# Nine projection tiles of a gated-linear-attention layer, computed by tokens in Strassen's scheme with GpSimd forming the weight sums

## The reference, cut to what matters

```python
def gla_branch(h, w_in, w_gate_up, gate_bias, out_norm_w):
    q, k, v, r, z, xq = split_cols(h @ w_in, [512, 512, 2048, 16, 3072, 1024])
    g = log_sigmoid(r @ w_gate_up + gate_bias) / 16
    o = gla_chunked(q * 128 ** -0.5, k, v, g)     # 4 heads, causal, state 128 x 512
    return rms_norm_2(o, out_norm_w), z, xq

# per layer:
xa = memory_attention(xq, mem_n, w_kv)
y = concatenate([seq_out, xa], -1) * silu(z)
x = x + y @ w_out
```

## Time and profile before

| | us |
|---|---|
| median of 3 runs | 1570.79 (1570.35 to 1570.9) |
| the profiled execution's own time | 1573.19 |
| its span, first to last instruction | 1571.4 |
| PE busy | 1522.5 (97%) |
| DVE busy | 656.8 (42%) |
| ACT busy | 288.3 (18%) |
| POOL busy | 82.2 (5%) |

### The profile page before, as it was taken

One profiled execution on the slowest core, in us unless ns is written; L12 is line 12 of the kernel. 1 busy time (PEld: TensorE's weight loads), 2 busy tenths in 40 slices (PEclk: granted clock), 3 DMA queues, 4 the chain that ended last, 5 costly groups with the idle time before them and its releaser, 6 DMA issues. The chain is left out here.

```text
span 1571.4 us, 22409 instructions
## 1 busy us (share of the span) xinstructions
PE 1522.5 (97%) x9037; PEld 973.5 (62%) x9037; DVE 656.8 (42%) x1262; ACT 288.3 (18%) x550; POOL 82.2 (5%) x125
## 2 busy tenths in 40 slices
PE   6999999999999999999999999998999999899998
PEld 2475655434434443443445788887888887488887
DVE  2544324111111111112311213473788888895663
ACT  2222202111212111112121020101232232240000
POOL 0000000000000000000100000001122122000000
PEclk9999999999999999999999999998999999999999
DMA  9544639899999999999333243334344344233441
GB/s 398 210 161 161 269 131 417 336 422 422 422 422 422 422 421 422 421 422 414 118 115 119 95 161 139 129 134 164 135 167 166 138 154 178 98 135 127 164 168 50
DMA packets 53889, 376.03 MB, mean 239 GB/s; under 512 B 7216, under 2 KB 18224, under 8 KB 19264
## 3 DMA queue, kind: packets, MB, share of 16 engines
q1 hardware_dynamic: 53536, 374.02, 59.9%
q10 hardware_dynamic: 288, 1.11, 0.2%
HBM read 373.99 MB, written 1.11 MB: 239 GB/s over the span
## 5 line engine op out<-in xcount | busy, mean ns | idle before, releaser
L1246 PE MATMUL ps<-ring,x_gathered 128*64 128x512 f32 x1024 | 227.4, 597 | 0.9 <-DVE x_gathered L1311 0.9
L1320 DVE TENSOR_TENSOR act_slots<-gate,ps 64x512 f32<-64x512 f32 x32 | 22.1, 690 | 380.8 <-ACT gate L1284 380.8
L2203 PE MATMUL ps<-hT,ring 128*128 128x256 f32 x768 | 173.6, 385 | 1.8 <-PEq L115 1.8
L1246 PEld LDWEIGHTS ps<-ring,x_gathered 128*64 128x64 f32 x1024 | 74.0, 138 | 148.3 <-issue 148.3
L2203 PEld LDWEIGHTS ps<-hT,ring 128*128 128x128 f32 x768 | 146.0, 193 | 23.8 <-issue 4.1
L1269 PE MATMUL ps<-ring,act_turned 128*64 128x512 f32 x512 | 116.9, 598 | 0.0
L1764 PE MATMUL ps<-hT,ring 128*128 128x256 f32 x512 | 111.4, 379 | 0.0
L1764 PEld LDWEIGHTS ps<-hT,ring 128*128 128x128 f32 x512 | 97.0, 190 | 14.7 <-issue 1.7
L1759 PE MATMUL ps<-ring,hT 128*128 128x512 f32 x192 | 85.6, 604 | 2.1 <-PEq L115 2.1
L1269 PEld LDWEIGHTS ps<-ring,act_turned 128*64 128x64 f32 x512 | 33.9, 136 | 79.1 <-issue 54.8
L1224 PE MATMUL ps<-y,selT 64*128 64x512 f32 x264 | 75.0, 634 | 0.7 <-ACT y L1290 0.7
(11 more groups left out here) (597 smaller groups left out, 2054.6 us busy)
## 6 DMA issues: line engine op xcount, KB each, us to landing
ring<-in_experts SPq DMA_DIRECT2D x192, 1024.0 KB, 15.7
ring<-in_weights SPq DMA_DIRECT2D x75, 2048.0 KB, 7.9
b_raw<-in_s_b SPq DMA_DIRECT2D x16, 128.0 KB, 7.1
s_a_rows<-s_ab_rows SPq DMA_DIRECT2D x64, 32.0 KB, 6.5
c_raw<-in_s_c SPq DMA_DIRECT2D x16, 128.0 KB, 6.1
b_by_state<-in_s_b_by_state SPq DMA_DIRECT2D x16, 128.0 KB, 2.0
x<-in_x ACTq DMA_DIRECT2D x1, 1024.0 KB, 4.9
mix_room<-in_mem SPq DMA_DIRECT2D x1, 1024.0 KB, 14.1
```

The costliest lines, as they stand in the source:

```text
L1246: last = pe.matmul(h_ps[rows, :], xg[:, f, :], w[:, kk, m, :], start=(f == 0), stop=(f == KD - 1))
L1320: dve.tensor_tensor(act_s[:], gate[:], h_ps[upper, :], ALU.mult).then_inc(act_ready, 1)
L2203: last = pe.matmul(out[:, f, :], w[:, kk, (2 * h + f) * P:(2 * h + f + 1) * P], rhs[:, kk, :], start=(kk == 0), stop=(kk == KD - 1))
```

## The change

Tiles 1 to 9 of the GLA projection are computed by a new class `TokenTiles`, by tokens, in Strassen's scheme. Tile 0 stays a plain tile by tokens, tiles 10 to 13 stay by features. The method `dve_weights` is renamed `sum_weights` and takes an engine; for the nine tiles that engine is POOL, for the other Strassen tiles it stays DVE.

```diff
+class TokenTiles(Strassen):        # fresh = 3, weight sums in zT, row sums in gla_xqT
+    def dve_rows(self, dve):
+        dve_row_sums(dve, self.rows_of(), self.row_sums).then_inc(self.rows_ready, 1)
+    def pe_first(self, pe, i):
+        self.k.wait_tile(pe, self.first + i)
+        pe.wait_ge(self.rows_ready, 1)
+        pe.wait_ge(self.weights_ready, i)
+        if i > 1:
+            pe.wait_ge(self.c11_out, i - 1)
+        self.pe_products(pe, i, 0, ("p1", "p6"), True).then_inc(self.part_done, 1)
+        if i > 1:
+            pe.wait_ge(self.rest_out, i - 1)
+        self.pe_products(pe, i, 1, ("p7", "p5"), True).then_inc(self.part_done, 1)
+    def pe_second(self, pe, i):
+        pe.wait_ge(self.u2_out, i)
+        self.pe_products(pe, i, 0, ("p2",), False).then_inc(self.part_done, 1)
+        pe.wait_ge(self.c22_out, i)
+        self.pe_products(pe, i, 1, ("p4", "p3"), False).then_inc(self.k.tile_done, 1)
+    def act_p1(self, act, i):
+        act.wait_ge(self.part_done, 3 * i - 2)
+        act.activation(self.one, self.ps(0, 0), ACT.Copy).then_inc(self.p1_out, 1)
+    def act_c11(self, act, i):
+        act.wait_ge(self.part_done, 3 * i)
+        act.activation(self.quarters(i)[0], self.ps(0, 0), ACT.Copy).then_inc(self.c11_out, 1)
+    def dve_u2(self, dve, i):
+        dve.wait_ge(self.p1_out, i)
+        dve.tensor_tensor(self.two, self.one, self.ps(0, 1), ALU.add).then_inc(self.u2_out, 1)
+        dve.drain()
+    def dve_c22(self, dve, i):
+        dve.wait_ge(self.part_done, 3 * i - 1)
+        dve.tensor_tensor(self.three, self.two, self.ps(1, 0), ALU.add)
+        dve.drain()
+        dve.tensor_tensor(self.quarters(i)[3], self.three, self.ps(1, 1), ALU.add).then_inc(self.c22_out, 1)
+    def dve_rest(self, dve, i):
+        dve.wait_ge(self.k.tile_done, self.first + i + 1)
+        dve.tensor_tensor(c21, self.two, self.ps(1, 0), ALU.add)
+        dve.tensor_tensor(c12, self.two, self.ps(1, 1), ALU.add).then_inc(self.rest_out, 1)
+        dve.drain()
```

Banks 6 and 7 hold [128, 256] twice each. `pe_products` issues 4 matmuls of 256 columns per product. In the lists of the engines:

```diff
 # tensor
-                half(2)
-                half(3)
-                half(4)
+                pe.wait_ge(out_dve, 2)
+                tiles.pe_first(pe, 1)
+                tiles.pe_second(pe, 1)
+                tiles.pe_first(pe, 2)
                 pe.wait_ge(g_ready, 1)          # then L1805 to L1809
...
-                half(5)
-                half(6)
-                half(7)
+                tiles.pe_second(pe, 2)
+                tiles.pe_first(pe, 3)
+                tiles.pe_second(pe, 3)
                 pe.wait_ge(dec_ready, 1)        # then the transposes of q and k
...
-                half(8)                         # before the scores
+                tiles.pe_first(pe, 4)
...
-                for i in range(9, 12):
-                    half(i)
+                tiles.pe_second(pe, 4)
+                tiles.pe_first(pe, 5)
+                tiles.pe_second(pe, 5)
                 pe.wait_ge(att_ready, 1)
-                pe.wait_ge(out_act, 12 - DVE_HALVES)
+                pe.wait_ge(tiles.c11_out, 5)
+                pe.wait_ge(tiles.rest_out, 5)
...                                              # updates, first(6), intra(0), second(6), intra(1), inter(1)
-                half(14)
-                for i in range(15, 22):
-                    half(i)
+                for i in range(7, TM_END):      # TM_END = 10
+                    tiles.pe_first(pe, i)
+                    tiles.pe_second(pe, i)
+                half(20)
+                half(21)
                 for r in range(2):
-                    pe.wait_ge(o_normed, 1)
+                    pe.wait_ge(gated, r + 1)
 # gpsimd
+                for i in range(1, TM_END):
+                    tiles.sum_weights(pool, i)
                 pool.wait_ge(summed, 8)         # the reciprocal root of o
 # scalar
+                tiles.act_p1(act, 1)
                 act.wait_ge(abs_ready, 1)
                 act.activation(lg, lg, ACT.Exp, scale=-1.0)
                 act.drain()
                 act.activation(lg, lg, ACT.Ln, bias=1.0).then_inc(log_ready, 1)
-                take(4)
+                tiles.act_c11(act, 1)
+                tiles.act_p1(act, 2)
...
-                for i in range(5, 16):
-                    take(i)
+                tiles.act_c11(act, 2)
+                for i in range(3, 8):
+                    tiles.act_p1(act, i)
+                    tiles.act_c11(act, i)
...                                              # squares of o, then p1(8), Silu of z tiles 6 to 9 in place,
...                                              # with c11(8), p1(9), c11(9) among them
 # vector
+                tiles.dve_rows(dve)              # first in the list
                 take(0)
...
-                take(2)
+                tiles.dve_u2(dve, 1)
                 dve.wait_ge(log_ready, 1)
                 ...                              # L1965, L1967 -> g_ready
-                take(3)
+                tiles.dve_c22(dve, 1)
+                tiles.dve_rest(dve, 1)
+                tiles.dve_u2(dve, 2)
+                tiles.dve_c22(dve, 2)
                 dve.wait_ge(exp_done, 1)
                 dve.scalar_tensor_tensor(out=q, in0=q, ..., in1=eq[:], ...)
+                tiles.dve_rest(dve, 2)
+                dve.wait_ge(tiles.c11_out, 1)
                 dve.tensor_tensor(ek[:], key, ek[:], ALU.mult)
                 dve.drain()
                 dve.tensor_tensor(key, key, lg, ALU.mult).then_inc(dec_ready, 1)
                 dve.memset(att, 0.0)
+                tiles.dve_u2(dve, 3)
...
-                last.then_inc(o_normed, 1)       # after the 8 products of L2005
+                for m in range(4):               # o * silu(z), by tokens, [128, 1024] each
+                    o = v[:, :, m * 512:(m + 1) * 512]
+                    dve.wait_ge(z_silu, m + 1)
+                    last = dve.tensor_tensor(o, o, z_tm[m], ALU.mult)
+                    if m % 2:
+                        last.then_inc(gated, 1)
                 for r in range(2):
-                    dve.tensor_tensor(z, z, fm(lo), ALU.mult).then_inc(z_ready, 1)
+                    dve.tensor_copy(zT[:, 8 * r:8 * r + 8, :], fm(lo)).then_inc(z_ready, 1)
```

More of the change, by code:

```diff
@@ L1563, in pe_turn, with __init__, rows_of, ps @@
         last.then_inc(turned, 1)
+class TokenTiles(Strassen):
+    def __init__(self, k, name, first, src, row_sums, weight_sums, quarters, spare):
+        super().__init__(k, name, first, weight_sums, 3)
+        self.src, self.row_sums, self.quarters = src, row_sums, quarters
+        self.one, self.two, self.three = spare
+        (self.rows_ready, self.part_done, self.p1_out, self.c11_out, self.u2_out, self.c22_out, self.rest_out) = (
+            k.sem(f"{name}_{n}") for n in ("rows_ready", "part_done", "p1_out", "c11_out", "u2_out", "c22_out", "rest_out"))
+    def rows_of(self):
+        return [self.src[:, 4 * j:4 * j + 4, t * P:(t + 1) * P] for t in range(TT) for j in range(2)]
+    def ps(self, bank, h):
+        return self.k.ps[:, 6 + bank, TOK * h:TOK * h + TOK]
+    def dve_rows(self, dve):
+        dve_row_sums(dve, self.rows_of(), self.row_sums).then_inc(self.rows_ready, 1)
+    def pe_products(self, pe, i, bank, products, start):
+        factors = self.factors(i, self.rows_of(), self.row_sums)
+        for h, p in enumerate(products):
+            rows, w = factors[p]
+            for kk in range(4):
+                last = pe.matmul(self.ps(bank, h), rows[:, kk, :], w[:, kk, :], start=(start and h == 0 and kk == 0),
+                                 stop=(kk == 3), skip_group_check=True)
+        return last
+    def pe_first(self, pe, i):
[29 more added lines that the diff above has]
+    def dve_rest(self, dve, i):
+        _c11, c12, c21, _c22 = self.quarters(i)
+        dve.wait_ge(self.k.tile_done, self.first + i + 1)
+        dve.tensor_tensor(c21, self.two, self.ps(1, 0), ALU.add)
+        dve.tensor_tensor(c12, self.two, self.ps(1, 1), ALU.add).then_inc(self.rest_out, 1)
+        dve.drain()
@@ L1901, in take, with silu @@
                     act.activation(half_dst(i), half_bank(i), ACT.Silu if i in Z_HALVES else ACT.Copy).then_inc(out_act, 1)
+                def silu(i):
+                    act.wait_ge(tiles.rest_out, i)
+                    act.drain()
+                    act.activation(tm[i], tm[i], ACT.Silu).then_inc(z_silu, 1)
+                tiles.act_p1(act, 1)
                 act.wait_ge(abs_ready, 1)
@@ L1918, in _ @@
                         i = 4 * t + h
-                        act.activation(junk[:], v[:, t, h * 512:(h + 1) * 512], ACT.Square,
+                        act.activation(eq[:, 0, :], v[:, t, h * 512:(h + 1) * 512], ACT.Square,
                                        accum_out=ss[:, i:i + 1]).then_inc(summed, 1)
                         act.drain()
-                for i in range(16, HALVES):
+                tiles.act_p1(act, 8)
+                for i in range(6, TM_END):
+                    silu(i)
+                    if i < 8:
```

(17 more changed lines are left out.)

123 lines of the change are left out of this document (71 added, 52 removed).

## The result

| | before | after |
|---|---|---|
| median of the runs, us | 1570.79 (1570.35 to 1570.9) | 1562.42 (1558.38 to 1563.43, 4 runs) |
| ratio, 95% interval | | 0.9939 [0.9927, 0.9952] |
| profiled execution, us | 1573.19 | 1563.43 |
| start of tile 1 to start of half 20, us | 781.62 to 932.35: 150.73 | 782.05 to 924.31: 142.26 |

8.4 us were gained where 11.4 were forecast: the time is inside the range, 3.0 above the point. It lies inside one trace, while whole executions of one kernel differ by several us (before: 1568.5 to 1573.6 over the experiments' runs) and tile 1 alone began anywhere from 776.5 to 782.05 us in the profiled executions, though PE's list ahead of it is the same in all of them.

A forecast was written before the change was run, and what follows sets the result against it. PE, busy 97% of the span, was taken as the bound. 15.6 us shed less waits of 1.8, 2.2 and 0.2 left 11.4, so 1570.8 - 11.4 = 1559.4 us; range 1556.6 to 1563.2.

The forecast's parts named there:

- What PE sheds: Tiles 1 to 9 on PE: 18 plain halves, 124.4 us, become nine Strassen tiles, 108.8; 15.6 us go.
- Rival C: The two-bank handover costs more than c22's spare, 0.3 to 0.5 more a tile: 1562 to 1564 us; 15%.
- c22's spare of 0.5: In each Strassen tile c22 is ready at 8.1 us and needed at 8.64: the tightest helper.
- Wait 1: Tile 1: c22 queued on DVE behind log_ready, done at 792.1 where PE asks at 790.3; 1.8 us lost.
- Wait 2: Tile 3: u2 late because two DVE products and POOL's sum 4 hold each other up; 2.2 us lost.
- Rival D: No contention between DVE and POOL ahead of tile 3's u2, so 2.2 us less: 1557.2 us; 13%.
- POOL's sums: Weight sums of [128, 1024] on POOL: 2.54 us each, 10.5 a tile with drains, hidden within 12.09 a tile.
- rival B: POOL sets the pace with sums over 3 us; even 3.3 costs 3 us, at tiles 8 and 9: 1562.5; 8%.
- Rival A: DVE's quarter sums with PSUM input also wait for POOL: 34 us lost for 15.6 gained, 1589 us; 4%.
- Wait 3: After tile 5 PE waits 0.9 for rest(5), where it waited 0.78 for ACT before: 0.2 us lost.
- the end of the stage: DVE's gating ends near 930, before PE wants it at 934.8: hidden, spare 5 us or more.
- The start of the stage: Sums 1 and 2 on POOL and DVE's row sums end about 773, before tile 1 at 781.6: free.

The follow-up runs named there:

- the products apart: Changed kernel with u2(3) between DVE's two products of exp_k and k, c22(3) behind the second, the memset last: 1561.58 us, ratio 0.9939.
- POOL held back: Changed kernel with POOL's sum 4 waiting until the two DVE products of exp_k and k are done: 1557.84 us, ratio 0.9908.
- both orders: Changed kernel with c22(1) ahead of DVE's log wait and u2(3) between the two DVE products: 1555.09 us, ratio 0.9887.
- first half of tile 6 ahead: The version with both orders, plus first(6) ahead of the state updates, second(6) behind them, first(7) between the two outputs: 1552.83 us, ratio 0.9887.

## Why the prediction was nearly right, and where it failed

- **What PE sheds, 15.6.** Right. Tiles 7 to 9 took 888.05 to 924.31, 36.26 against 36.3, without idle time, and the stretch with only tiles 1 to 5 in the scheme came out as reckoned. Rival C is out: c22's spare of 0.5 held in every tile but the first, where c22 stood behind the log.
- **Wait 1, taken as 1.8: the step that failed.** It was 3.1 in idle time and 1.8 more in slow products. The order of queues was read rightly (c22 behind log_ready), but the step took the Exp's table load as done, since before shows just the second load beside the Exp. The load belongs to the instruction behind it and moved with it: 1.3. The clock was not weighed at all. The experiments on this wait gave 4.1 and 4.9 us, so in this trace the term is 4.9 instead of 1.8, 3.1 more and the whole of the miss. Of these, 1.3 could have been read from the trace of before, by the load at 760.35; the 1.8 of the clock doesn't come with every such gap, as the last section shows.
- **Wait 2, taken as 2.2: 1.5.** Mechanism right, shown by holding POOL back. The size: the sum on POOL is 2.35, near the lower bound of 2.28, with which the working gave 1.7. Rival D is out.
- **POOL's sums, taken as 2.54: 2.35**, and 9.65 a tile instead of 10.5, so rival B is out; a sum more a tile cost 0.7, two cost 7.1. The Trainium skill, "GPSIMD Engine Reference", section "3.1 Elementwise — side-by-side cycle accounting", by its 2.6 cycles gave an estimate of 2.2 to 2.3; the trace is just above it.
- **Rival A is out**: quarter sums from PSUM at 0.42 beside POOL.
- **Wait 3, 0.2: 0.2**, and the end of the stage was hidden as reckoned: DVE's last gating product ran from 931.57 to 932.8, PE wanted it at 938.12.
- **The start of the stage** was free, though DVE's row sums took 2.67 to 2.84 us each beside POOL and 0.69 with POOL idle (the sums on DVE): both were done by 773.
- Errors set against each other: -3.1 at wait 1, +0.7 at wait 2, -0.5 in first products: -2.9, and the stretch gained 8.5 instead of 11.4.
- **The range held in part by luck.** By the working's own bounds, those of the POOL sum, the time was to be 1558.9 to 1560; 1562.4 lies outside them. The range went up to 1563.2 for rivals B and C, and the runs show neither. What filled that room was wait 1, which had no bounds of its own.

## What to carry to other kernels

When an instruction is put into ACT's list ahead of an activation that has a table load, count the load as part of that activation: it waits behind the newcomer, however long the engine was idle. A gap on a full TensorE can cost more than its length, so a spare of half a microsecond is fine in a steady run of tiles, but the one place where its helper stands behind a long wait should be reordered first: one call moved here gave 4.1 or 4.9 us, where the whole change had given 8.5. Price contention by whole operations of the other engine, taken in turn.

## What the runs showed of the hardware

- **Short gaps and the clock.** After the gap of 2.9 us in tile 1 the mean granted clock of the next 5 us was 0.50 to 0.66, and two products took 1.8 to 3.05 us more, in all four traces with that gap (the change, the products apart, POOL held back, tiles 1 to 5); after 2.18 at tile 4 with two sums more, they took 1.75 more. After 2.95 at tile 9 of that same trace it stayed at 1.00, and in the stretch after none of the gaps up to 1.4. Nor does the place decide it. Every trace has one and the same gap of 2.1 us ahead of tile 0, in code that no version changes. In eight of the twelve the clock is down behind it and tile 0's first 16 instructions take 8.8 us; in four (the products apart, both orders, first half of tile 6 ahead, one sum more) it is at 1.00 and they take 7.1. The change, then the products apart:
```profile
760.83 8.77 PE L1841 MATMUL ps<-ring,hT 128*128 128x512 f32 x16 [2.12 <-PEq L115]
```
```profile
759.22 7.11 PE L1841 MATMUL ps<-ring,hT 128*128 128x512 f32 x16 [2.12 <-PEq L115]
```
So a gap of 2 to 3 us in full work costs some 1.7 to 3 us more in some executions and nothing in others. What decides is open, and whether every run of the changed kernel paid the 1.8 at tile 1 isn't shown.
- **DVE and POOL, both ways.** Where a DVE operation with two inputs in SBUF met POOL's sums, each waited for one operation of the other: DVE 1.22 became 2.69 and 3.22, POOL 2.35 became 3.15 and 3.35. With one input in PSUM DVE kept its 0.42 beside the same sums.
